# A two-layer hybrid decoder step on Trainium2: norms summed and spread on PE tiles, a longer ring of column buffers, pooling on four tiles

## What is computed

```
h = rmsnorm(x, norm_g); proj = h @ w_in          # one projection, split into the parts below
lru_x, lru_z, nsa_q, nsa_kv, nsa_z, nsa_g, dn_qkv, dn_z, dn_a, dn_b, merge_g
RG-LRU:     u = conv4(lru_x); r, i = sigmoid(u @ wa + ba), sigmoid(u @ wx + bx)
            a = exp(8 r log_sigmoid(lam)); h_t = a h_(t-1) + sqrt(1 - a^2) (i u);  out = (h * silu(lru_z)) @ w_lru_out
attention:  q = rope(rmsnorm_64(nsa_q) * q_norm) / 8 ; k = rope(rmsnorm_64(k) * k_norm)   # 8 heads, 2 kv heads of 64
            compressed blocks of 32 (mean), selected blocks of 64 (top 16), window of 512; gates sigmoid(nsa_g)
            out = (o * silu(nsa_z)) @ w_nsa_out
DeltaNet:   qkv = silu(conv4(dn_qkv)); q = l2norm(q) / sqrt(128); k = l2norm(k)         # 4 heads of 128
            chunks of 64 with a triangular solve, state S; o = rmsnorm_128(o) * o_norm
            out = (o * silu(dn_z)) @ w_dn_out
merged = sum over branches of sigmoid(merge_g) * out;  x = x + merged @ w_out
```

## Time and profile before

| | |
|---|---|
| median of 3 runs | 2050.67 us (2050.65 to 2054.24) |
| the profiled execution | 2052.01 us |
| its span | 2050.2 us |
| mean granted TensorE clock | 0.98 |
| PE busy | 1949.3 us (95%) |
| DVE, ACT busy | 754.2 us (37%), 567.3 us (28%) |

### The profile page before, as it was taken

The page is one execution under the profiler, slowest core; times in us unless marked ns, Lnnn a source line. Parts: engine busy times, 40 slices in busy tenths (PEclk is TensorE's granted clock), DMA queues, the critical chain, the costliest instruction groups (busy, mean ns, idle before and its releaser), DMA issues.

```text
span 2050.2 us, 28883 instructions
## 1 busy us (share of the span) xinstructions
PE 1949.3 (95%) x11470; PEld 1411.3 (69%) x11470; DVE 754.2 (37%) x1866; ACT 567.3 (28%) x1203; POOL 80.5 (4%) x116
## 2 busy tenths in 40 slices
PE   6999899997999999999999898999979999999999
PEld 4777688885765567777467676888857655777763
DVE  2447342413444434311124563433134553433110
ACT  4131412114356511100321333120152664111000
POOL 0000101001010000000000002010101000000000
PEclk9999999998999999999999999999999999999999
DMA  6212310112411136335032131010233111553401
GB/s 223 93 43 60 87 43 21 43 47 90 132 51 32 42 102 199 102 104 170 0 151 79 42 94 55 22 43 22 67 107 113 32 31 46 164 173 92 160 31 46
DMA packets 182493, 166.78 MB, mean 81 GB/s; under 512 B 48272, under 2 KB 173634, under 8 KB 181846
## 3 DMA queue, kind: packets, MB, share of 16 engines
q1 hardware_dynamic: 178806, 147.93, 23.8%
q0 software_dynamic: 3552, 17.00, 2.2%
HBM read 151.44 MB, written 21.71 MB: 84 GB/s over the span
## 4 chain that ended last, share of the span: by engine, by line
PE 90%; ACT 4%; DVE 4%; issue 2%; DMA 0%; SPq 0%; DVEq 0%; ACTq 0%
PE PS L827 60%; PE PS L767 6%; PE PS L1198 2%; PE PS L1211 2%; PE PS L1006 1%; PE PS L1277 1%; PE PS L1024 1%; PE PS L1026 1%; PE PS L1267 1%; PE PS L1095 1%; PE PS L1143 1%; PE PS L936 1%; PE PS L909 1%; PE PS L1156 1%; PE PS L1117 1%
## 5 line engine op out<-in xcount | busy, mean ns | idle before, releaser
L827 PE MATMUL PS<-hT,ring 128*128 128x288 f32 x3968 | 1068.0, 414 | 29.2 <-ACT arena L1439 8.8
L827 PEld LDWEIGHTS PS<-hT,ring 128*128 128x128 f32 x3968 | 738.9, 193 | 241.4 <-issue 18.6
L827 PE MATMUL PS<-zs,owr 128*128 128x288 f32 x768 | 208.5, 408 | 0.0
L827 PEld LDWEIGHTS PS<-zs,owr 128*128 128x128 f32 x768 | 143.1, 190 | 39.3 <-issue 1.5
L767 PE MATMUL PS<-con,arena 128*128 128x128 f32 (+5 forms) x934 | 143.6, 279 | 18.2 <-DMA arena<-in_nsa_k_norm 12.8
L767 PEld LDWEIGHTS PS<-con,arena 128*128 128x128 f32 (+5 forms) x934 | 106.8, 139 | 78.1 <-issue 49.4
L827 PE MATMUL PS<-arena 128*128 128x512 f32 (+1 forms) x320 | 124.8, 593 | 2.1 <-issue 2.1
L1457 ACT ACTIVATE sg<-PS 128x288 f32<-128x288 f32 x96 | 38.7, 403 | 303.3 <-PE PS L827 303.3
L1779 DVE SCALAR_TENSOR_TENSOR mpr<-sg,PS 128x288 f32<-128x288 f32 x64 | 29.1, 454 | 208.7 <-PE PS L827 206.0
L1739 DVE SCALAR_TENSOR_TENSOR arena<-arena,par 128x512 f32<-128x512 f32 x192 | 99.5, 518 | 6.8
L827 PEld LDWEIGHTS PS<-arena 128*128 128x128 f32 (+1 forms) x320 | 52.7, 179 | 71.1 <-issue 70.9
(11 more groups left out here) (291 smaller groups left out, 1845.4 us busy)
## 6 DMA issues: line engine op xcount, KB each, us to landing
ring<-in_w_in SPq DMA_DIRECT2D x54, 1024.0 KB, 5.3
arena<-in_cache_nsa_kv SPq DMA_DIRECT2D x128, 192.0 KB, 2.6
ring<-in_w_in SPq DMA_DIRECT2D x32, 256.0 KB, 3.6
arena<-in_state_nsa_win SPq DMA_DIRECT2D x32, 256.0 KB, 3.2
arena<-in_cache_nsa_kv SPq DMA_DIRECT2D x128, 64.0 KB, 1.9
arena<-in_w_out SPq DMA_DIRECT2D x4, 2048.0 KB, 9.9
out_win_sample<-in_state_nsa_win POOLq DMA_DIRECT2D x2, 4032.0 KB, 22.9
arena<-in_x_prompt SPq DMA_DIRECT2D x8, 512.0 KB, 9.7
```

Of the source, the lines that this page charges most:

```text
L827: ins = mm(to, w, x, start=start, stop=stop, skip_group_check=True)
```

## The change

Five norms of several chunks replace the per-chunk ones: `dn` (DeltaNet q), `dn_k`, `o`, `k`, `q`. `square_sums` multiplies the squares with 128 x 32 weights (`sum`, or `sum2` for two heads of 64), chunk j on column group j, so that the sums of up to four chunks lie on 32 partitions each of one bank per half. ACT takes one Ln and one Exp of 128 x 576 for all of them. `broadcast` spreads the root: for each half four matmuls with 32 rows of `spread`, one on each row group, write banks 4 to 7, and DVE multiplies straight from PSUM (`times_roots`). Signals are ms_ok, ln_ok and rstd_ok (5 a layer), bc_ok and bm_ok (10 a layer: five norms in two halves). The o, k and q norms stand together now, ahead of the silu of DeltaNet's gates and of dn_ok.

Further edits: the ring of `dext` grows from 3 to 7 buffers; ACT takes evictions between the Tanh and the Exp of the LRU; softplus and the DeltaNet gate (gb_ok) stand before the first convolution of this layer; the input norm uses Sqrt on ACT and a reciprocal on DVE instead of Ln and Exp; the small parameters of layer 0 are loaded over ACT's queue, not SyncE's; the pooling of keys and values uses four column groups of 128 columns instead of two of 256.

```diff
-EXTN = 3
+EXTN = 7
...
+            def square_sums(past, norm, w, squares):
+
+                at, count = NORMS[norm]
+                pe.wait_ge(s["sq_ok"], past["sq_ok"] + SQ[norm])
+                if at:
+                    pe.wait_ge(s["ln_ok"], past["ln_ok"] + at)
+                for h in range(2):
+                    for j in range(count):
+                        ins = mm(PS[32 * j:32 * j + 32, 2 + h, 0:HALF], C(w), hh(squares[:, j], h), start=True, stop=True,
+                                 skip_group_check=True)
+                step("ms_ok")
+                ins.then_inc(s["ms_ok"], 1)
+
+            def broadcast(past, norm, roots, h):
+
+                at, count = NORMS[norm]
+                pe.wait_ge(s["rstd_ok"], past["rstd_ok"] + at + 1)
+                if at or h:
+                    pe.wait_ge(s["bm_ok"], past["bm_ok"] + 2 * at + h)
+                for j in range(count):
+                    r = slice(32 * j, 32 * j + 32)
+                    ins = mm(PS[:, 4 + j, 0:HALF], C("spread")[r], hh(roots[r], h), start=True, stop=True)
+                step("bc_ok")
+                ins.then_inc(s["bc_ok"], 1)
...
-                for n in range(8):
-                    fill(4, u0 + U_MG0)
-                    pe.wait_ge(s["sq_ok"], past["sq_ok"] + SQ["dn"] + n + 1)
...
+                fill(8, u0 + U_MG0)
+                square_sums(past, "dn", "sum", dsq[:, 0:4])
+                fill(8, u0 + U_MG0)
+                square_sums(past, "dn_k", "sum", dsq[:, 4:8])
+                fill(12, u0 + U_MG0)
+                for norm, n in (("dn", 0), ("dn_k", 4)):
                     for h in range(2):
...
+                        fill(5, u0 + U_MG0)
+                        broadcast(past, norm, dsq[:, n], h)
                 fill(8, u0 + U_MG0)
-                pe.wait_ge(s["n_ok"], past["n_ok"] + 8)
+                pe.wait_ge(s["bm_ok"], past["bm_ok"] + 4)
...
-                for n in range(DN_H):
-                    fill(6, u0 + U_MG0)
...
+                fill(6, u0 + U_MG2)
+                square_sums(past, "o", "sum", dc[:, 4:8])
+                fill(8, u0 + U_MG2)
+                square_sums(past, "k", "sum2", rs7[:, 4:7])
+                fill(8, u0 + U_MG2)
+                square_sums(past, "q", "sum2", rs7[:, 0:4])
+                fill(12, u0 + U_MG2)
+                for norm, roots in (("o", dc[:, 4]), ("k", rs7[:, 4]), ("q", rs7[:, 0])):
                     for h in range(2):
...
+                        fill(5, u0 + U_MG2)
+                        broadcast(past, norm, roots, h)
                 dense_to(u0 + U_MG0)
...
-                for n in range(7):
-                    pe.wait_ge(s["sq_ok"], past["sq_ok"] + SQ["qk"] + n + 1)
...
-                    fill(3, u0 + U_MG2)
...
+                pe.wait_ge(s["bm_ok"], past["bm_ok"] + 10)
...
-                        for b2 in range(2):
-                            ins = mm(PS[32 * b2:32 * b2 + NPB, 5, 0:2 * P], con[:, at:at + NPB], page(b2, k)[:, 0:2 * P],
+                        for i in range(4):
+                            ins = mm(PS[NPB * i:NPB * (i + 1), 5, 0:P], con[:, at:at + NPB],
+                                     page(i % 2, k)[:, i // 2 * P:(i // 2 + 1) * P],
...
                 for c in range(4):
+                    if c % 2 == 0:
+                        take_to(u0 + U_DC + 6 + c // 2)
                     A(lt[:, c], la[:, c], ACT.Tanh, scale=lamn[:, 0, c:c + 1])
                 for c in range(4):
+                    if c % 2 == 0:
+                        take_to(u0 + U_DC + 8 + c // 2)
                     ins = A(la[:, c], la[:, c], ACT.Exp, scale=lamn[:, 1, c:c + 1])
...
+                for n in range(4, 7):
+                    A(rs7[:, n], qk7[:, n], ACT.Square).then_inc(s["sq_ok"], 1)
+                log_of("o", dc[:, 4], 1.0 / DN_D)
+                for n in range(4):
+                    A(rs7[:, n], qk7[:, n], ACT.Square).then_inc(s["sq_ok"], 1)
+                log_of("k", rs7[:, 4], 1.0 / HD)
+                log_of("q", rs7[:, 0], 1.0 / HD)
+                root_of("o", dc[:, 4])
+                root_of("k", rs7[:, 4])
+                root_of("q", rs7[:, 0])
+                take_before("bc_ok", 10)
                 take_to(u0 + U_MG0)
                 act.wait_ge(s["pa"], taken(u0 + U_MG0, "A"))
                 A(zs[:, 8:12], zs[:, 8:12], ACT.Silu).then_inc(s["silu_ok"], 1)
...
-                act.wait_ge(s["dn_ok"], past["dn_ok"] + 1)
...
+                for h in range(2):
+                    times_roots("o", h, dc[:, 0:4], prm("on")).then_inc(s["bm_ok"], 1)
...
+                    times_roots("q", h, qk7[:, 0:4], prm("qn")).then_inc(s["bm_ok"], 1)
                 take_to(u0 + U_MG0)
...
+                dve.wait_ge(s["bm_ok"], past["bm_ok"] + 10)
                 dve.wait_ge(s["silu_ok"], past["silu_ok"] + 4)
                 mul(zs[:, 8:12], zs[:, 8:12], dc[:, 0:4]).then_inc(s["dn_ok"], 1)
```

More of the change, by code:

```diff
@@ L76 @@
 ])
-NFIRST = CON["ones"][0]
+NFIRST = CON["sum"][0]
 def constants():
@@ L482, in _, with small_weights @@
             for k in range(4):
-                sp.dma_start(xr[k], dram["x_prompt"][0, k * P:(k + 1) * P, :]).then_inc(s[f"x_in{k}"], 16)
+                sp.dma_start(xr[k], dram["x_prompt"][0, k * P:(k + 1) * P, :]).then_inc(s[f"x_in{min(k, 2)}"], 16)
             x_s = dram["x_sample"].rearrange("b t c -> (b t) c")
             for f in range(2):
[L486 to L513, removed]
+                sp.dma_start(xr[4][f * T_S:(f + 1) * T_S], x_s[:, f * 512:(f + 1) * 512]).then_inc(s["x_in2"], 16)
+            def small_weights(l):
                 w_in = at_layer("w_in", l).rearrange("a (j p) c -> p (a j) c", p=P)
@@ L1562, in _ @@
                     A(dc[:, 4 + n], dc[:, n], ACT.Square).then_inc(s["sq_ok"], 1)
-                for n in range(DN_H):
-                    take_before("ms_ok", MS["o"] + n + 1)
-                    act.wait_ge(s["ms_ok"], past["ms_ok"] + MS["o"] + n + 1)
-                    A(halves(dc[:, 4 + n]), pair(4 + 2 * (n % 2)), ACT.Ln, bias=C("eps"), scale=1.0 / DN_D)\
-                        .then_inc(s["ln_ok"], 1)
-                act.wait_ge(s["ln_ok"], past["ln_ok"] + LN["o"] + DN_H)
-                A(dc[:, 4:8], dc[:, 4:8], ACT.Exp, scale=-0.5).then_inc(s["rstd_ok"], 1)
+                act.wait_ge(s["pv"], taken(u0 + U_KV, "V"))
+                take_before("b_pe", 3 + DN_H)
+                act.wait_ge(s["b_sn"], past["b_sn"] + DN_H)
+                for n in range(4, 7):
[9 more added lines that the diff above has]
+                take_before("bc_ok", 10)
                 take_to(u0 + U_MG0)
@@ L1573, in _ @@
                 A(zs[:, 4:8], zs[:, 4:8], ACT.Silu).then_inc(s["silu_ok"], 1)
-                act.wait_ge(s["pv"], taken(u0 + U_KV, "V"))
-                act.wait_ge(s["dn_ok"], past["dn_ok"] + 1)
-                for n in range(7):
-                    A(rs7[:, n], qk7[:, n], ACT.Square).then_inc(s["sq_ok"], 1)
-                for n in range(7):
-                    take_before("ms_ok", MS["qk"] + n + 1)
-                    act.wait_ge(s["ms_ok"], past["ms_ok"] + MS["qk"] + n + 1)
-                    A(halves(rs7[:, n]), pair(4 + 2 * (n % 2)), ACT.Ln, bias=C("eps"), scale=1.0 / HD)\
-                        .then_inc(s["ln_ok"], 1)
-                act.wait_ge(s["ln_ok"], past["ln_ok"] + LN["qk"] + 7)
-                A(rs7[:], rs7[:], ACT.Exp, scale=-0.5).then_inc(s["rstd_ok"], 1)
                 take_before("nq_sw", 7)
@@ L1708, in turned_rows @@
                             gains.rearrange("p (f c) -> p c f", f=2).unsqueeze(3).to_broadcast([P, 4, 2, n])).then_inc(s["h_ok"], 1)
+            for k in range(3):
+                row_root(0, k)
             parameters(0)
@@ L1712, in _ @@
                 turned_rows(0, k)
+            row_root(0, 3)
             for l in range(DEPTH):
@@ L2039, in _ @@
                 link(V.memset(exn[:], 0.0))
+                link(V.memset(cp2[:], 0.0))
                 def gate(qt, br):
```

212 lines of the change are left out of this document (111 added, 101 removed).

## The result

The changed kernel takes 2036.8 us (median of 4 runs, 2034.23 to 2039.83) against 2050.66 before; the ratio is 0.9928, 95% interval 0.9916 to 0.994. It is 13.9 us faster, where 29.7 was forecast. The time lies inside the stated range of 1999 to 2048, but outside the 2010 to 2033 that case A had for itself, and less than half of the gain came. The profiled execution is the slowest of the four, 2039.83 us with a span of 2038.0, so the two traces differ by 12.2 us.

What follows compares the result with a forecast made beforehand. TensorE, busy 95% of the span, was taken as the bound. Terms of 13.5 us per layer, 27.0 for two, 29.5 with the start, led from 2052.0 to 2022.5, as a median 2021 us; range 1999 to 2048.

Steps and rivals of the forecast that it cites:

- case A: Whole kernel: the main forecast with all its terms, 2021 us, own range 2010 to 2033, chance 0.64.
- start, once: Kernel start: Sqrt with DVE's reciprocal needs no table loads between, saving two of 1.28 us: +2.5 us once.
- LRU and convolution: LRU and convolution stage: two PE stalls, 3.3 and 4.4 us, go with their restarts: +10.7 us a layer.
- DeltaNet norms and restart: DeltaNet q/k norms: cheaper square sums and broadcasts, 7.8 us scaling stall and its restart gone: +12.8 us a layer.
- end of DeltaNet: Last state additions: the stream ends early, so PE has nothing to put under them: -1.5 us a layer.
- o, k, q norms and the ring wait: Norms before attention: PE reaches first key transposes early, stalls 22 us for weights issued behind dn_ok: -5.0 us a layer.
- attention: Attention: 69 fillers left instead of 112, 14 of 36 pairs unfilled, 0.77 us idle each: -10.8 us a layer.
- pooling: Pooling of cached keys: a burst falls from 3.65 to 1.8 us on four column groups: +7.3 us a layer.
- rival D: Broadcasts: the four row groups run one after another, 1.95 us each, about 2046 us in all, chance 0.06.
- Rivals B and C: First: no new stall, ring weights in time, 1973, chance 0.08; second: attention loses only 2 to 4 us, about 2006, 0.14.
- Rival E: ACT among the norms: gates' units need table reloads, dn_ok 16 us later a layer, about 2055 us, slower, chance 0.08.

Runs made afterwards that it cites:

- the DeltaNet fillers alone: Changed kernel with 12 fewer filler matmuls in the DeltaNet norms only (12 to 4, 8 to 4), SyncE's order unchanged: 2022.6 us, ratio 0.9857.
- slot 21 early: Changed kernel with one weight-ring slot and its output weights issued by SyncE ahead of its wait for dn_ok: 1994.2 us, ratio 0.9703.
- the moved wait: Changed kernel with PE's wait for the last scaling (bm_ok 10) placed behind the rotation's first four fillers instead of ahead: 2037.3 us.
- fewer fillers: Changed kernel with fewer fillers in norm stages, rotation and transposes, wait for last scaling behind one filler group, SyncE's order kept: 1996.1 us, ratio 0.9734.
- both together: Changed kernel with the early ring slot and output weights plus the reduced fillers, attention's 102 spread evenly: 1955.3 us, ratio 0.954.

## Why the prediction was wrong

**What held.** Layer 0, at equal work, in us (forecast, measured):

| step | forecast | measured |
|---|---|---|
| start, once | +2.5 | +1.6 |
| LRU and convolution | +10.7 | +11.3 |
| DeltaNet norms and restart | +12.8 | +11.6 |
| end of DeltaNet | -1.5 | -2.7 |
| o, k, q norms and the ring wait | -5.0 | -10.8 |
| attention | -10.8 | -12.2 |
| pooling | +7.3 | +6.8 |
| sum | +16.0 | +5.6 |

The measured column is the differences of one chain of places: 1.6 at the start of the stream, 12.9 at 203.80, 24.5 at the second L986 (16.7 of time and 16 matmuls), 21.8 at the last state addition (18.4 of time and 7 matmuls), 11.0 at 579.10 (43 matmuls, less 10.0 of time), 0.5 at the end of attention with 1.7 of pooling in it. Layer 1 has +6.6 in all, 24.1 for the first two steps, -4.3 and -8.9 for the next two, -11.1 in attention. The mechanisms are those forecast, the new wait among them: 22 us were predicted for it, 21.5 and 22.3 came. That its length agrees so well is partly luck: PE came to position 720 at T = 70.9 and not at 65.7, and the weights at 92.4 and not at 87.7, and the two errors nearly cancel in the wait, though not in the sum. The price of a broadcast, 0.70, is exact, so rival D, the serial row groups, falls. By an estimate from the figure of the Trainium skill (TensorE: Matmul & The Clock Gate, LDWEIGHTS) the eight loads would be 0.86 one after another; the trace, 0.70 with everything, decides against such a sum. A square sum is 1.10 for 1.2. Rivals B and C fell by their own signs: the wait came, and the pairs pay. Rival E falls as well, since dn_ok came at 49.5 and not past 60, but a small piece of what it describes is in the trace, as the next part shows.

**The step that failed** is the term "o, k and q norms", which was mis-sized: -5.0 against -10.8 and -8.9 a layer, 9.7 of the 17.3 us that are missing between the profiles (29.5 forecast, 12.2 measured); 4.0 are missing at the end of DeltaNet, the other 3.6 in small pieces at the start, in attention and in the pooling. The form of the step was right, that dn_ok sets when PE goes on. Its time was wrong: dn_ok at T = 45, measured 49.5 (520.80 less the last state addition's end, 471.27). Since all behind it is fixed, the weights landed at 92.4 for 87.7, and each of these 4.7 us went into the sum. The windows of two stretches show where the larger part comes from, 6.1 us after the state additions at a granted clock of 0.50, and the same level behind the ring wait:

```profile
471.30:477.40 6.10, 6.08 (x15) 3.89 (x16) 0.00 (x0) 3.11 (x4) 1.77 (x1) 0.50 0.56 204
563.60:567.80 4.20, 4.17 (x9) 2.95 (x10) 0.00 (x0) 0.00 (x0) 0.00 (x0) 0.50 1.09 385
```

The run with the DeltaNet fillers alone, where dn_ok came at the counted T = 45.0, tells what the 4.5 us consist of. There the first square sum begins 3.65 us behind the last addition, here 6.11, so 2.5 more: the twelve records of 0.243 behind it took 6.1 us instead of 2.9. The other 2.0 are a wait which stands in the rows of the norms stage above, 1.77 us at 483.47, and which that run does not have. PE waits there for the eviction of a gates' unit, which ACT does behind the Ln of the o norm, four squares and a table load:

```profile
479.31 2.39 ACT L1599 ACTIVATE arena<-arena 128x576 f32<-128x576 f32 x4
481.72 1.28 ACT L1470 ACT_TABLE_LOAD   x1
483.01 0.41 ACT L1470 ACTIVATE sg<-PS 128x288 f32<-128x288 f32 x1
```

This is rival E's mechanism in one place. The 1.5 us wait for the last scaling is no part of it, since dn_ok waits for that scaling in any case. The forecast had the wait for the last addition (1.39 us) in its -1.5, but had not asked what clock PE would have behind it, and it had put the eviction wait at nothing. The restart behind the ring wait was 3.1 us (8 records in 4.18, 6 transposes in 1.49, 8 records in 2.50), not 1.9: 4.7 and 1.2 are the 5.8 of the table within rounding. One part is a slip of addition: 45 + 1.0 + 35.9 + 5.3 are 87.2, where the forecast has 87.7, so its own terms give -4.5 for this step and the weights came 5.2 later than they say.

The 4.0 us that are missing at the end of DeltaNet lie mostly in one stretch, 64 matmuls of 16 columns (L1095 before, L1123 now) and the twenty records behind them. It took 14.9 us before in both layers and takes 16.5 and 18.1 now, 1.6 and 3.3 more. PE was busy all the time; the granted clock differs (first the kernel before, then the changed one, each layer 0):

```profile
456.12:471.00 14.88, 14.88 (x85) 13.04 (x84) 1.10 (x2) 0.41 (x1) 5.89 (x4) 0.77 0.19 55
439.40:455.90 16.50, 16.50 (x85) 14.46 (x83) 1.10 (x2) 0.41 (x1) 6.30 (x4) 0.69 0.00 1
```

The half clock is not the same in every execution: the twelve records took 6.13 us here, 4.75 with slot 21 early, 4.71 in layer 1, and 3.18 in the run with the moved wait, all behind the same wait of 1.4 us, and dn_ok moved with them (T = 49.5, 48.1, 48.1 and 46.5). What decides it these runs don't say; it may be part of why this kernel's times scatter by 5.6 us. So some of the shortfall is the luck of the execution: with the 3.18 us stretch dn_ok would have been 1.5 us late and not 4.5.

**What the change as a whole teaches.** The three parts that add no wait, buffers, order of evictions and pooling, give 24 (the first two together) and 14 us alone. By addition that is 38, which was not run as one kernel, and more than the whole change with its 13.9. The rest, the new norms and their place above all, wins in the DeltaNet stage and still costs 24 us by this difference, by where they stand and how many fillers stand among them. The runs with fewer fillers and with the slot early take 41 and 43 us back, and both together 82.

What stays open: what decides the clock behind a short wait and in the narrow matmuls, why the eviction wait is gone when twelve fillers stand a stage later, the 1.6 to 2.7 us of attention that the fillers don't explain, and whether the o, k and q norms in the old order with the new form would be better still, which was not run.

## What to carry to other kernels

Where one in-order queue serves two users, look for what is now reached earlier than what releases the queue: a stage made faster ahead of such a wait only makes the wait longer when the release stays where it is (in layer 1 1.5 us won, 1.4 us waited), and two issues put ahead of the release were worth 43 us. Fillers are a stock: a filler put where no wait is has to be missed somewhere else, and here 43 a layer moved cost 22 us in a kernel otherwise unchanged. When you price a short stall of TensorE, price the clock behind it too, and the release that hangs on the stretch behind it.

## What the runs showed of the hardware

- Four matmuls of 32 x 128 weights on four row groups, 288 columns, two passes: 0.70 us from start to start with the change of form; eight of 128 x 32 on four column groups: 1.10 us.
- Behind one wait of 1.4 us the granted clock was 0.50 for 6.1 us in one execution, and in another, with the same wait and the same program up to there, it stayed at 1.00:

```profile
470.96:474.10 3.14, 3.14 (x16) 2.23 (x17) 0.00 (x0) 3.09 (x4) 1.77 (x1) 1.00 0.15 53
```

This is the window behind the state additions in the run with the moved wait.

- In 64 matmuls of 16 columns and the work behind them the granted clock was 0.77 before and 0.69 and 0.62 in the two layers of the changed kernel, though PE shows no idle time there.
- In the run with the moved wait, attention took 140.3 us in layer 0 at a granted clock of 0.94, and 136.7 in layer 1 at 0.99, with the same matmuls and the same share of the stream.
